# Attention of the first layer: two-map heads' units first, latent heads' units last, and output units that start on the two-map heads' K tiles

## The reference, cut to what matters

```python
mod = silu_c @ w_ada + b_ada                       # 6 vectors of 2048: shifts, scales, gates
h = modulate(rmsnorm(x, g_norm_mix), shift_m, scale_m)
proj = h @ w_in                                    # 2048 x 3904
dq, dk, dv, q_lat, kv_lat, k_pe = jnp.split(proj, IN_SPLITS, axis=-1)
...
# 8 two-map heads: two softmax maps each, subtracted
a = softmax(q1 k1) - lam * softmax(q2 k2);  o_diff = rmsnorm(a @ dv, g_diff_sub) * c
# 8 latent heads: queries, keys and values come out of normed latents
q  = rmsnorm(q_lat, g_q_a) @ w_q_b                 # 512 x 1536
kv = rmsnorm(kv_lat, g_kv_a) @ w_kv_b              # 256 x 2048
o_mla = softmax(q_nope k_nope + q_rope k_rope) @ v
mix = concatenate([o_diff, o_mla]) @ w_out         # 2048 x 2048
x = x + gate_m * mix                               # then norm, feed-forward, second layer
```

## Time and profile before

| | |
|---|---|
| median of 3 executions | 2119.35 us (2119.01 to 2122.26) |
| profiled execution, its own time | 2116.66 us |
| its span in the trace | 2114.6 us |
| TensorE / VectorE / ScalarE / GpSimd busy | 94% / 62% / 45% / 6% |
| DMA | 448.83 MB, mean 212 GB/s |

### The profile page before, as it was taken

How to read it: one execution, slowest core, us unless ns; L and a number is a source line. 1 busy time by engine, 2 the same in 40 slices (tenths; PEclk the granted TensorE clock), 3 DMA queues, 4 the chain that set the end, 5 groups by cost and what they waited for, 6 DMA issues and landing times. The chain is left out here.

```text
span 2114.6 us, 24917 instructions
## 1 busy us (share of the span) xinstructions
PE 1980.5 (94%) x9272; PEld 1631.5 (77%) x9272; DVE 1315.1 (62%) x2079; ACT 941.6 (45%) x1436; POOL 129.4 (6%) x94
## 2 busy tenths in 40 slices
PE   6798896869899999999999999989999999999999
PEld 3377775548778888888888878889998788888887
DVE  3888776788796555555555556567665555545554
ACT  2554445434544344444434455455444444444442
POOL 0000000002000110110010022010000001101000
PEclk9899998979999999999999999999999999999999
DMA  9997675759797555555555545534544456656654
GB/s 361 382 376 263 241 254 187 249 188 343 273 356 267 194 200 188 190 192 184 191 191 188 186 160 182 188 112 144 164 134 145 132 159 199 189 189 196 192 189 169
DMA packets 128969, 448.83 MB, mean 212 GB/s; under 512 B 14289, under 2 KB 14545, under 8 KB 128337
## 3 DMA queue, kind: packets, MB, share of 16 engines
q1 hardware_dynamic: 124928, 433.74, 60.4%
q0 software_dynamic: 1568, 7.34, 0.9%
q10 hardware_dynamic: 2352, 6.17, 0.8%
HBM read 443.00 MB, written 4.19 MB: 211 GB/s over the span
## 5 line engine op out<-in xcount | busy, mean ns | idle before, releaser
L1724 DVE TENSOR_TENSOR wlo<-raw,whi 128x1024 fp32r<-128x1024 f32 (+4 forms) x554 | 659.4, 1193 | 593.4 <-ACT whi L1511 568.4
L1511 ACT ACTIVATE whi<-raw 128x1024 fp32r<-128x1024 f32 (+4 forms) x554 | 557.0, 1007 | 708.2 <-PE g L1386 638.4
L1381 PE MATMUL g<-whi,lhsA_hi 128*128 128x512 f32 (+4 forms) x1840 | 713.6, 389 | 27.7 <-issue 13.7
L1382 PE MATMUL g<-whi,lhsA_lo 128*128 128x512 f32 (+4 forms) x1840 | 693.5, 379 | 0.0
L1386 PE MATMUL g<-wlo,lhsA_hi 128*128 128x512 f32 (+4 forms) x1840 | 463.7, 374 | 0.0
L1381 PEld LDWEIGHTS g<-whi,lhsA_hi 128*128 128x128 f32 x1840 | 354.9, 193 | 91.9 <-issue 33.1
L1382 PEld LDWEIGHTS g<-whi,lhsA_lo 128*128 128x128 f32 x1840 | 354.9, 193 | 53.3 <-issue 1.7
L1386 PEld LDWEIGHTS g<-wlo,lhsA_hi 128*128 128x128 f32 x1840 | 339.2, 190 | 54.6
L1381 PE MATMUL g<-whi,lhsF_hi 128*128 128x512 f32 x512 | 200.6, 392 | 0.0
L1382 PE MATMUL g<-whi,lhsF_lo 128*128 128x512 f32 x512 | 199.4, 389 | 0.0
L1729 DVE SCALAR_TENSOR_TENSOR raw<-raw,srow 128x1024 f32<-128x1024 f32 x147 | 178.0, 1236 | 19.2 <-DMA raw<-in_w_ada 19.0
(11 more groups left out here) (270 smaller groups left out, 1559.4 us busy)
## 6 DMA issues: line engine op xcount, KB each, us to landing
raw<-in_w_ff SPq DMA_DIRECT2D x182, 512.0 KB, 3.6
raw<-in_w_in SPq DMA_DIRECT2D x161, 512.0 KB, 3.9
raw<-in_w_ada SPq DMA_DIRECT2D x147, 512.0 KB, 5.1
region<-in_w_ff SPq DMA_DIRECT2D x74, 512.0 KB, 4.1
raw<-in_w_out SPq DMA_DIRECT2D x60, 512.0 KB, 5.1
raw<-in_w_in SPq DMA_DIRECT2D x80, 384.0 KB, 3.1
region<-in_w_ada SPq DMA_DIRECT2D x34, 512.0 KB, 5.9
region<-in_w_in SPq DMA_DIRECT2D x15, 512.0 KB, 7.9
```

Source lines behind the costliest of these rows:

```text
L1381: eng.matmul(o, p.xh[:, kk, t * P:t * P + P], h, start=p.first and kk == 0, stop=False)
L1382: eng.matmul(o, p.xl[:, kk, t * P:t * P + P], h, start=False, stop=False)
L1511: eng.activation(p.hi, p.raw, ACT.Copy).then_inc(p.hi_done[0], 1)
L1724: eng.tensor_tensor(p.lo, p.raw, p.hi.bitcast(F32), ALU.subtract).then_inc(p.lo_done[0], 1)
```

## The change

`order1` puts all six units of the two-map heads first, in the order in which heads 0 to 3 and then heads 4 to 7 become possible, and the four latent units after them. `diff_end` for both groups is put into the background list right behind the heads, not after the loop. The first two output units begin with K blocks 8 to 15 (two-map heads) and end with 0 to 7 (latent heads).

```diff
-    order1 = (("h", 2), ("h", 3), ("l", 0), ("h", 0), ("l", 1), ("h", 4), ("l", 2), ("l", 3), ("h", 1), ("h", 5))
+    order1 = (("h", 2), ("h", 0), ("h", 4), ("h", 3), ("h", 1), ("h", 5), ("l", 0), ("l", 1), ("l", 2), ("l", 3))
...
-    u_out = units([("w_out", 512 * i, 512, (0, 8), lhsA) for i in range(2)])
-    for u, v in zip(u_out, units([("w_out", 512 * i, 512, (8, 8), lhsA) for i in range(2)])):
-        u["tiles"], u["pairs"] = u["tiles"] + v["tiles"], list(range(8))
+    u_out = units([("w_out", 512 * i, 512, (8, 8), lhsA) for i in range(2)])
+    for u, v in zip(u_out, units([("w_out", 512 * i, 512, (0, 8), lhsA) for i in range(2)])):
+        u["tiles"], u["pairs"], u["k_off"] = u["tiles"] + v["tiles"], [4, 5, 6, 7, 0, 1, 2, 3], 0
...
+            if len(halved) == 6:
+                lhsA.ready[4:8] = [None] * 4
+                bg.append(diff_end(0))
+                bg.append(diff_end(1))
...
-    lhsA.ready[4:8] = [None] * 4
     bg.append(spread(0, gate_free))
-    bg.append(diff_end(0))
-    bg.append(diff_end(1))
```

## The result

The changed kernel takes 2142.56 us (median of 4 executions, 2140.36 to 2146.11), the kernel before beside it 2119.18 (2118.41 to 2122.26). The ratio is 1.0109, its 95% interval 1.009 to 1.0128. I had forecast 2113 and a range up to 2127. The profiled execution took 2144.4 us, span 2142.5; that is 27.9 above the span of before.

The account below looks back on a forecast made before the run. Chains over three engines, not one full engine, were taken as the bound. Stretches and round 48 summed to 247.4 against 255.5 us, 8.1 less; plus 2 for late tiles gave 2110.6, as median 2113.3 us, range 2103 to 2127.

Parts of the forecast that it names:

- A4: Rounds 65 to 71, two-map heads 4 to 7 beside latent units, twelve w_ada tiles: 51 us (45 to 56).
- slower rival: Latent units' pairs too short beside head chains in rounds 65 to 71: 64 us there, 2126 in all; chance 0.18.
- A2: Rounds 53 to 59, seven 512-column pairs, two-map heads 0 to 3, seven w_ada tiles: 42 us (36 to 46).
- A3: Rounds 60 to 64, five pairs and the latents' turning: 23.3 us (20 to 24).
- A5: Rounds 72 to 76, five pairs, both diff_end and rotated rows: 30 us (28 to 34).
- A6: Rounds 77 to 83, seven 512-column pairs and all eight latent heads: 60 us (52 to 63).
- A7: Rounds 84 to 88, five pairs, last latent results split, four gates: 26 us (24 to 30).
- third stretch: Kernel before, two-map heads 0 to 3 between latent units and latent heads: counted 47.2 us, measured 73.98, excess 26.8.
- The late tiles: From round 89 each w_ada tile comes three pairs later; 2 us lost ahead of the feed-forward, between 0 and 3.4.
- The x load: Load on GpSimd's queue, now behind round 88, starting some 2.4 us later: costed at nothing, at most 2 us.
- The clock: Rounds 65 to 71 at the low clock throughout: 53 us of TensorE work, 2 above the forecast value.
- A1: Rounds 49 to 52, four pairs, no excess: 12 us.

Follow-up runs that it names:

- after_rounds: Changed kernel with ADA_LEFT rewritten so each round from 49 on reduces as many w_ada tiles as in the kernel before: 2123.03 us, ratio 1.0016.
- shortened tiles: w_ada reductions of rounds 49 to 88 done over 8 columns instead of 512: kernel before 2086.72 us (0.9841), changed kernel 2105.95 us (0.9932).
- thinned table: Changed kernel, tiles by round as before, then w_ada tiles of rounds 65 to 76 cut from 23 to 8 by ADA_LEFT: 2130.43 us, ratio 1.0053.
- one_step: Changed kernel, tiles by round as before, with steps=1 instead of 2 for the w_kv_b pairs: 2126.06 us, ratio 1.0031.
- before_late3: Kernel before, with ADA_LEFT entries from the end of the stage on moved three pump calls later: 2132.02 us, ratio 1.0056.
- table3: Changed kernel, with ADA_LEFT entries from the end of the stage on moved three pump calls earlier: 2136.53 us, ratio 1.0072.
- after_lean: Changed kernel, tiles by round as before, then 23 w_ada tiles of rounds 65 to 76 cut to 8, the others placed elsewhere: 2130.43 us, ratio 1.0053.
- spacing: Changed kernel, tiles by round as before, one more yield in diff_end between normalisation and transposes: 2131.7 us; another also in each two-map head: 2130.62 us.

## Why the prediction was wrong, point by point

**The step that failed** is the count of the stretches: the greater of the two engines' work, plus an excess taken from before. Its worst term is A4's excess of 14, "nearer the lower". The runs show 22.9 in the changed kernel (59.8 on 36.9) and 24.4 with the tiles by round as before (61.3 on 36.9), just where I had set the point from which the slower rival decides; A2's excess of 11 was 16. With the tiles by round as before (after_rounds) the stage is 259.8 us from round 49 on, and not the 244.3 of my sum: A2 5.4, A3 2.1, A4 10.3, A5 2.6 and A6 1.2 over it, A7 5.9 under it.

Two things make it so. First, a `w_ada` tile among two-map heads is paid nearly in full: 0.83 us in A2 and 0.95 in A4 by the shortened tiles, 1.2 in A4 by the thinned table, 1.0 to 1.2 in the old order's third stretch. My count hides a tile wherever TensorE has more work. In A2 it charged 2.3 us for seven tiles (31.2 on VectorE against 28.9 on TensorE), and they cost 5.8. In A4 this was not the fault: VectorE was the fuller engine in my count, so its twelve tiles were charged with 10.3 (36.9 against 26.6), and they cost 11.4. Second, and this is A4's, the chains themselves cost more there: with shortened tiles A4 is 48.4 us on 26.6 of TensorE work, 21.8 over it, and A2 with the same number of heads 41.3 on 28.9, 12.4 over. So the slower rival's reason, that chains beside latent units are dearer, holds for some 9 us. In one_step A4 lost 5.1 us and A5 gained them, so the double call of `pump` isn't what makes the two dear together, and whether the short pairs or the rotated rows do stays open. The old order had the like in its third stretch (59.5 on 41.0), so it isn't what made the change slower.

**The second failure** is most of what the change lost against the kernel before: I saw that the new order makes three calls of `pump` fewer, and looked for the consequence behind round 89 alone. Inside the stage the same shift moves the table against the rounds too, and that costs 11.5 of the 16.2 us (9.1 in the old order). I had given each stretch its number of tiles and never looked at which instruction they stand in front of.

**The sum** has a slip beside that. Round 48 "without the latents' turning" was set at 3.1 us, its pair included, against 6.1 before; but that row starts at 235.12, behind the pair (the pair starts at 232.28). In the same terms the new value is 0.4 (235.61 to 235.97), so the working should have given 244.7 for the stage and 2110.6 for the median, further still from what came. Three readings are off as well, without weight in the sum: in the seventh slice of the earlier trace rows VectorE is at 6 tenths, the DMA share starts at 0.44 in the earlier trace rows, and by the count VectorE is the fuller engine in five of the seven stretches and not in four.

**The late tiles** were priced at 2 us, at most 3.4, with the argument that by 583 us both orders had reduced the same number. Up to the first feed-forward pair they cost 3.8 (before_late3), and then the `lhsA` rows wait on: table3's 6 and before_late3's 12 us are the measure. The number reduced by a certain time is no price; what counts is which tile a row waits for.

**The x load** was costed at nothing, 2 at most: the pairs show a wait of 1.13 us at 528.04 in the changed kernel, and none in after_rounds, whose A7 holds five tiles instead of ten. Place and mechanism were right: the cover is gone in the kernel in which VectorE comes late out of the stage. VectorE's row there, which waits for GpSimd:

```profile
525.12 0.69 DVE L1937 TENSOR_TENSOR tmp<-g,region 128x512 f32<-128x512 f32 x1 [6.62 <-POOL region L2116]
```

**The clock** "adds no case of its own": wrong. From round 49 to 88, the changed kernel and after_rounds:

```profile
235.97:507.26 271.29, 202.71 (x919) 158.51 (x917) 191.90 (x407) 113.96 (x288) 0.00 (x0) 0.86 0.59 207
```

```profile
237.35:497.18 259.83, 196.29 (x919) 154.23 (x918) 193.92 (x414) 113.46 (x288) 0.00 (x0) 0.88 0.64 220
```

The same 919 TensorE instructions are 6.4 us longer busy, of the 11.5 between the two. A clock that falls behind stalls isn't a rival to the waits but a factor on them.

**What held:** A1, A3 and round 48, from its pair's start, to within 0.6 us; exponential waits of at most 3.8 us between two-map heads; three tiles ahead of the first `lhsA_lo`. The latents' splitting did not: 5.8 us in two waits instead of 3.6. Of the signs of being wrong, the latent units' seven rounds stayed just under 60 us, but the latent heads' rounds did wait for copies, 7.4 us in four. The Trainium skill's rule on interleaving regimes ("Perfetto Trace Analysis", Optimization Strategy), by which I had set a positive sum beside mine, has the right sign: with the tiles by round as before the order that separates the two kinds of head is 4 us slower (3.4 by the ratio, 1.5 to 5.5 by its interval). The runs show it as a small effect here. Where those 4 us lie is only argued, from the trace: the transposes of the early `diff_end` wait 10.5 us for `diff_norm` in two waits where one of 3.2 stood before, since rotated rows, a `wlo` and tiles stand between its two steps on VectorE. That spacing didn't remove the wait leaves the point open.

## What to carry to other kernels

Filler work that a table releases by a count of calls belongs to the order of everything else: whoever reorders the work must place the filler again, and compare two orders only at equal placement. A filler instruction in an in-order queue costs nothing beside bare products as long as the fetches keep up (13 tiles in rounds 89 to 108 of after_rounds, TensorE never idle), and nearly its full length ahead of a step of a dependent chain, however idle its engine is on average. Before filler is moved into an engine's idle time, the DMA share of that stretch has to be looked at too. And a stall of TensorE is to be priced with the lower clock that follows it.

## What the hardware showed

VectorE's elementwise instructions are longer while GpSimd adds: in after_lean two of 1.22 us take 1.94 and 2.31 beside a GpSimd pair of 3.52.

```profile
512.30 3.52 POOL L2118 TENSOR_TENSOR region<-region,tmp 128x512 f32<-128x512 f32 x2 [6.76 <-DVE tmp L1939]
```

```profile
512.74 1.94 DVE L1727 TENSOR_TENSOR wlo<-raw,whi 128x1024 fp32r<-128x1024 f32 x1
514.60 2.31 DVE L1732 SCALAR_TENSOR_TENSOR raw<-raw,srow 128x1024 f32<-128x1024 f32 x1
516.83 1.22 DVE L1727 TENSOR_TENSOR wlo<-raw,whi 128x1024 fp32r<-128x1024 f32 x1
```

From round 89 to the feed-forward the 20 tiles in `raw` buffers take 1.38 us on average there and 10 such tiles 1.32 in after_rounds, against 1.22 in the stage, so this adds little to what the moved tiles cost. The Trainium skill ("SBUF — State Buffer", Who interferes with whom) gives the two engines one shared pair of ports, held by one instruction at a time; the rows agree in that two instructions with two inputs each lose together 1.8 us to one GpSimd pair.
